# A transformer kernel on one core: the passage from its first block to its second, with norm factors applied behind the products, six weight slots from an earlier place, and the memory's operands made beside the gates

## The reference

```python
        x = x + y @ w_out[i]
        gate = jax.nn.sigmoid(rms_norm(x, ple_norm_g[i]) @ ple_w_gate[i])
        x = x + gate * (p[i] @ ple_w_proj[i])
    return rms_norm(x, final_norm_g)                 # end of the first block
...
        h = rms_norm_2(x, attn_norm[l])              # second block, layer 0: NSA attention
        proj = h @ w_in
...
    kv = (rms_norm_2(mem, g_mem) @ w_mem_kv).reshape(B, M, 2, N_MEM_HEADS, HEAD_DIM)   # for both layers
```

## Time and profile before

| | us |
|---|---|
| three runs | 1324.72, 1329.7, 1330.0; median 1329.7 |
| the profiled execution, its own time | 1329.96 |
| its span on the core | 1328.2 |
| TensorE busy in the span | 1142.6 |
| VectorE, ScalarE, GpSimd busy | 964.5, 692.3, 151.7 |
| mean granted TensorE clock | 0.924 of full speed |

### The profile page before, as it was taken

The page is one execution under the profiler, slowest core; times in us unless marked ns, Lnnn a source line. Parts: engine busy times, 40 slices in busy tenths (PEclk is TensorE's granted clock), DMA queues, the critical chain, the costliest instruction groups (busy, mean ns, idle before and its releaser), DMA issues.

```text
span 1328.2 us, 24918 instructions
## 1 busy us (share of the span) xinstructions
PE 1142.6 (86%) x10403; PEld 1062.7 (80%) x10403; DVE 964.5 (73%) x1722; ACT 692.3 (52%) x1261; POOL 151.7 (11%) x113
## 2 busy tenths in 40 slices
PE   6799876979799758948976699999999959999997
PEld 6688765969678748848965599999999848999997
DVE  5787954666778855577768867888867576788873
ACT  5642256555532366555345845565655274565562
POOL 2000000110000001142000001223110000123210
PEclk9999986989899967978986989999999879999999
DMA  8332110344231103415530034554556403455461
GB/s 340 127 100 93 65 64 1 135 151 157 90 128 66 65 1 142 139 69 186 179 128 25 1 129 157 173 177 159 199 203 211 150 1 101 156 173 175 159 207 63
DMA packets 24736, 167.54 MB, mean 126 GB/s; under 512 B 2737, under 2 KB 2865, under 8 KB 8497
## 3 DMA queue, kind: packets, MB, share of 16 engines
q1 hardware_dynamic: 24624, 165.96, 35.8%
HBM read 164.90 MB, written 1.05 MB: 125 GB/s over the span
## 4 chain that ended last, share of the span: by engine, by line
PE 48%; DVE 29%; ACT 17%; issue 4%; DMA 2%; POOL 0%; DVEq 0%; SPq 0%; ACTq 0%; POOLq 0%
PE ps L427 9%; PE ps L422 9%; PE ps L424 9%; DVE WL L381 8%; ACT WH L368 3%; DVE FR L381 3%; PE ps L445 3%; PE ps L453 3%; PE ps L447 3%; ACT ARENA L745 2%; PE ps L643 2%; DMA raw<-wst_in 2%; ACT FR L368 1%; ACT ARENA L2136 1%; ACT L484 1%
## 5 line engine op out<-in xcount | busy, mean ns | idle before, releaser
L381 DVE TENSOR_TENSOR WL<-raw,WH 128x1024 fp32r<-128x1024 f32 (+4 forms) x225 | 274.0, 1240 | 104.6 <-ACT WH L368 104.0
L422 PE MATMUL ps<-FR,WH 128*128 128x256 f32 x1248 | 305.3, 285 | 21.8 <-ACT WH L368 16.5
L424 PE MATMUL ps<-FR,WH 128*128 128x256 f32 x1248 | 301.2, 282 | 1.3 <-DVE FR L493 0.8
L368 ACT ACTIVATE WH<-raw 128x1024 fp32r<-128x1024 f32 (+4 forms) x225 | 218.3, 988 | 101.8 <-PE ps L427 55.4
L422 PEld LDWEIGHTS ps<-FR,WH 128*128 128x128 f32 x1248 | 240.4, 193 | 26.9 <-ACT WH L368 13.6
L424 PEld LDWEIGHTS ps<-FR,WH 128*128 128x128 f32 x1248 | 240.0, 192 | 3.2 <-DVE FR L493 1.9
L422 PE MATMUL ps<-FR,FR 128*128 128x256 f32 x680 | 169.1, 286 | 2.9 <-ACT FR L368 2.2
L427 PE MATMUL ps<-FR,WL 128*128 128x256 f32 x1248 | 170.1, 279 | 0.5 <-DVE WL L381 0.5
L424 PE MATMUL ps<-FR,FR 128*128 128x256 f32 x680 | 167.9, 284 | 0.2 <-DVE FR L493 0.2
L427 PEld LDWEIGHTS ps<-FR,WL 128*128 128x128 f32 x1248 | 155.7, 189 | 0.7 <-DVE WL L381 0.7
L381 DVE TENSOR_TENSOR FR<-raw,FR 128x1024 fp32r<-128x1024 f32 (+2 forms) x100 | 127.3, 1297 | 34.5 <-ACT FR L368 34.5
(11 more groups left out here) (320 smaller groups left out, 1825.9 us busy)
## 6 DMA issues: line engine op xcount, KB each, us to landing
raw<-wst_in SPq DMA_DIRECT2D x124, 1024.0 KB, 5.0
raw<-wst_in SPq DMA_DIRECT2D x14, 768.0 KB, 4.2
raw<-wst_in SPq DMA_DIRECT2D x11, 896.0 KB, 4.7
raw<-wst_in SPq DMA_DIRECT2D x4, 968.0 KB, 4.7
raw<-wst_in SPq DMA_DIRECT2D x2, 912.0 KB, 4.6
cst<-cst_in SPq DMA_DIRECT2D x1, 1681.0 KB, 15.3
X<-xT_in SPq DMA_DIRECT2D x2, 512.0 KB, 6.3
ARENA<-memT_in SPq DMA_DIRECT2D x1, 1024.0 KB, 4.8
```

The costliest lines, as they stand in the source:

```text
L368: a.activation(hi[:, 0:cols], src, ACT.Copy).then_inc(*put("split_hi", ("hi", i)))
L381: v.tensor_tensor(lo[:, 0:cols], src, hi[:, 0:cols].bitcast(F32), SUB).then_inc(*put("split_lo", ("lo", i)))
L422: pe.matmul(out, hv[:, k, :], src.hi[:, c, :], start=k0 == 0 and k == ks[0], stop=False)
L424: pe.matmul(out, hv[:, k, :], src.lo[:, c, :], start=False, stop=False)
```

## The change

1. **Factors behind the products.** The operand of the NSA projections is X times `g12`, the product of the two gains (final norm and attention norm), without row factors. It is split in the gate pairs of layer 1 (`HN`). The row factor of both norms, `rs12`, is multiplied in where the projections leave PSUM (as a column `rT12`, or as a row for `zc`). The memory's operands are M times its gain, its factor `mem_rs` is multiplied into the keys, and as a column into the values. Two small steps (`columns_pe`, `columns_v`) turn a row factor into a column. `scaled` is no longer used here, and GpSimd makes no parts.
2. **The memory's operands** for both layers are made in gate pairs 0 and 2 of layer 1: 16 `hi` on ScalarE, 16 `lo` on VectorE.
3. **Memory products first.** Keys of layer 0, mean of X, values of layer 0, keys of layer 1, second mean, values of layer 1, then the projections.
4. **Six slots** begin with the first `w_out` item of layer 1, before with the first item of the projections; so splits run 5 items ahead through `w_out` and the gates of layer 1.
5. **One `w_proj` item** of 1024 columns holds the weights of four outputs, in both layers; before, each output had its own of 256. The list of items has 314 entries in 157 tiles, before 326 in 159.
6. Buffers move in the arena: `M` lies at 2048, the operands at the end of `OutMap`.

```diff
-MORE_AT = ("mem v", 1)
+MORE_AT = ("gate", 1, 4)
...
+        if j < NW:
+            return w_slots[j], max(x for x in range(m - NW, m) if x % NW == j)
...
-        ahead = ahead or (2 if n < first_more() else 4 if event[0] == "cmp1" else NW + NMORE - 1)
+        ahead = ahead or (2 if n <= first_more() else 4 if event[0] == "cmp1" else NW + NMORE - 1)
...
-            if i == first_more():
+            if i == first_more() + NW:
                 for e in ("PE", "V", "G"):
-                    q.wait_ge(*got("end", "T", e))
+                    q.wait_ge(*got("end", ("L", 1), e))
...
+    def proj_pe(l, c0, ps):
+
+        if c0 % 4 == 0:
+            proj_item[0] = take(("ple_w_proj", l, tuple(r(128 * c0, 128 * c0 + 512)), 0, 2), 1024)
+        i, hi, lo = proj_item[0]
+        hv, lv = (x.rearrange("p (k m) -> p k m", k=2) for x in (hi, lo))
+        src, tag = p_parts[l], ("p", l)
+        qpe.wait_ge(*got("hi", i))
+        qpe.wait_ge(*got("lo", i))
+        for x in range(2):
+            o, m = ps[:, 256 * x:256 * x + 256], slice(128 * (c0 % 4 + x), 128 * (c0 % 4 + x) + 128)
+            for k in range(2):
+                qpe.wait_ge(*got("hi", tag, k))
+                pe.matmul(o, hv[:, k, m], src.hi[:, k, :], start=k == 0, stop=False)
+                qpe.wait_ge(*got("lo", tag, k))
+                pe.matmul(o, hv[:, k, m], src.lo[:, k, :], start=False, stop=False)
+                ins = pe.matmul(o, lv[:, k, m], src.hi[:, k, :], start=False, stop=k == 1)
+        ins.then_inc(*put("item_used", ("w_proj", l, c0), *([("used", i)] if c0 % 4 else [])))
+        B.at_items["w_proj", l, c0] = len(B.plan)
...
+        if l == 1 and c0 < 4:
+            for i in range(2):
+                for c in r(2 * c0, 2 * c0 + 4):
+                    part_x_lo(v, q, mem_parts[i], ("mem", i), c, vcol("mem_norm_2", i, 0, 8), M)
...
-            elif c0 == 4:
-                ps, free = psum("mem mean")
-                q.wait_ge(*got("mem y"))
-                newton(v, q, "mem_v", mem_rs, ps[:, 0:S], 1e-6, mem_hs[0], ("mem rs",), free)
-                q.wait_ge(*own("mem_v"))
-            elif c0 == 6:
-                for i in range(2):
-                    if i:
-                        q.wait_ge(*got("lo", ("mem", 0), 6))
-                        q.wait_ge(*got("lo", ("mem", 0), 7))
-                    scaled_v(v, q, M, vcol("mem_norm_2", i, 0, 8), mem_parts[i], ("mem", i), mem_hs, bank=mem_rs)
+            else:
+                if c0 == 0:
+                    v.tensor_tensor(g12, vcol("final_norm_g", None, 0, 8), vcol("attn_norm_2", 0, 0, 8), MUL).then_inc(*put("ple_v", ("g12",)))
+                q.wait_ge(*own("ple_v"))
+                for c in (c0, c0 + 1):
+                    part_x_lo(v, q, HN, "HN", c, g12)
...
-            if l == 1 and c0 == 4:
-                q.wait_ge(*got("mem mean"))
-                table(a, LNEXP)
-                ps, _ = psum("mem mean")
-                a.activation(mem_hs[0], ps[:, 0:S], ACT.Ln, bias=C("eps6")).then_inc(*put("mem_a"))
-                q.wait_ge(*own("mem_a"))
-                a.activation(mem_hs[0], mem_hs[0], ACT.Exp, scale=-0.5).then_inc(*put("mem_a", ("mem y",)))
+            if l == 1 and c0 < 4:
+                for i in range(2):
+                    for c in r(2 * c0, 2 * c0 + 4):
+                        part_x_hi(a, mem_parts[i], ("mem", i), c, vcol("mem_norm_2", i, 0, 8), M)
...
-            elif c0 < 4:
-                pass
-        if l == 1:
-            q.wait_ge(*got("mem mean"))
-            for c0 in range(0, 8, 2):
+            else:
+                q.wait_ge(*got("g12"))
+                for c in (c0, c0 + 1):
+                    part_x_hi(a, HN, "HN", c, g12)
+                if c0 == 4:
+                    q.wait_ge(*got("mem mean"))
                 a.activation(m.sq3[c0 // 2], X[:, c0:c0 + 2, :], ACT.Square).then_inc(*put("square", ("square", ("in", 2), c0)))
...
     def between_pe():
+        memory_k_pe(0)
         mean_mm(("in", 2), lo_[1].sq3[0])
-        memory_kv_pe(0)
+        memory_v_pe(0)
+        memory_k_pe(1)
+        columns_pe(mem_rs, "mem rT", "mem rs")
         mean_mm(("fin", 1), t_sq[0])
+        memory_v_pe(1)
+        columns_pe(rs12, "rT12", "rs12")
         B.mark("PE", "end", "T", "PE")
...
     def between_v(v, q):
         barrier(q, "V", ("O", 1))
-        rstd_v(v, q, ("in", 2), None, t_y0)
+        split_lo(v, q, "mem k", 0)
+        ps, free = psum("mem mean")
+        q.wait_ge(*got("mem y"))
+        newton(v, q, "mem_v", mem_rs, ps[:, 0:S], 1e-6, mem_y, ("mem rs",), free)
+        split_lo(v, q, "mem v", 0)
+        rstd_v(v, q, ("in", 2), rs1, t_y0)
         for c in range(KC):
-            v.scalar_tensor_tensor(X[:, c, :], X[:, c, :], vcol("final_norm_g", None, c), mean_bank[:, 0:S], MUL, MUL) \
-                .then_inc(*put("scaled", ("x fin", c), *([("mean free", ("in", 2))] if c == 7 else [])))
-        split_lo(v, q, "mem k", 0)
-        split_lo(v, q, "mem v", 0)
+            v.scalar_tensor_tensor(X[:, c, :], X[:, c, :], vcol("final_norm_g", None, c), rs1, MUL, MUL) \
+                .then_inc(*put("scaled", ("x fin", c)))
+        q.wait_ge(*got("mem rs"))
+        memory_k_v(v, q, 0)
+        split_lo(v, q, "mem k", 1)
+        columns_v(v, q, mem_rT, "mem rT")
+        split_lo(v, q, "mem v", 1)
+        rstd_v(v, q, ("fin", 1), rs12, t_y0)
+        v.tensor_tensor(rs12, rs12, rs1, MUL).then_inc(*put("rstd_v", ("rs12",)))
+        memory_k_v(v, q, 1)
+        columns_v(v, q, rT12, "rT12")
         B.mark("V", "end", "T", "V")
...
     def between_a(a, q):
         barrier(q, "A", ("O", 1))
+        ps, _ = psum("mem mean")
+        q.wait_ge(*got("mem mean"))
+        table(a, LNEXP)
+        a.activation(mem_y, ps[:, 0:S], ACT.Ln, bias=C("eps6")).then_inc(*put("mem_a"))
+        q.wait_ge(*own("mem_a"))
+        a.activation(mem_y, mem_y, ACT.Exp, scale=-0.5).then_inc(*put("mem_a", ("mem y",)))
+        split_hi(a, q, "mem k", 0)
         rstd_a(a, q, ("in", 2), t_y0)
-        split_hi(a, q, "mem k", 0)
+        split_hi(a, q, "mem v", 0)
         for c in range(0, KC, 2):
             q.wait_ge(*got("x fin", c + 1))
             a.activation(t_sq[c // 2], X[:, c:c + 2, :], ACT.Square).then_inc(*put("square", ("square", ("fin", 1), c)))
-        memory_kv_a(a, q, 0)
+        split_hi(a, q, "mem k", 1)
+        memory_v_a(a, q, 0)
+        split_hi(a, q, "mem v", 1)
+        rstd_a(a, q, ("fin", 1), t_y0)
+        memory_v_a(a, q, 1)
         B.mark("A", "end", "T", "A")
...
-        barrier(q, "V", "T")
-        split_lo(v, q, "mem k", 1)
-        rstd_v(v, q, ("fin", 1), None, m.zt[:, 0, 0:256])
-        scaled_v(v, q, X, vcol("attn_norm_2", 0, 0, 8), m.H, "HN", m.hs, ("fin", 1), mean_bank[:, 0:S])
-        split_lo(v, q, "mem v", 1)
...
+            v.tensor_scalar(dst, ps[:, 0:NSA_N[g]], rT12[:, 1:2], None, MUL).then_inc(*put("proj_v", ("zt n", g) if g < 2 else ("zv n", 1), free))
...
+            v.tensor_tensor(m.zc[:, c0:c0 + 2, :] if c0 < 4 else m.qm, two(ps), bc(rs12, 1, 2), MUL) \
+                .then_inc(*put("proj_v", ("zc a", c0) if c0 < 4 else ("qm",), free))
...
-        barrier(q, "A", "T")
-        split_hi(a, q, "mem k", 1)
-        rstd_a(a, q, ("fin", 1), m.zt[:, 0, 0:256])
-        scaled_a(a, q, m.H, "HN", m.hs)
-        memory_kv_a(a, q, 1)
+        q.wait_ge(*got("rT12", "v"))
```

108 lines of the change are left out of this document (57 added, 51 removed).

## The result

The changed kernel takes 1332.7 us (median of 18 runs, 1330.3 to 1335.2), the kernel before 1329.7 in the same runs (18, 1324.7 to 1333.4): ratio 1.0023, 95% interval 1.0013 to 1.0032. It is 3.0 us slower (1.7 to 4.3), a small loss, outside the -0.4 us that was forecast. The profiled execution took 1331.15 us, of which 1329.1 are span.

A forecast was written before the change was run, and what follows sets the result against it. TensorE was taken as the bound, waiting on VectorE and ScalarE's chain before the projections. Passage -1.6, U +1.2 and layer 0 at 0 gave -0.4 us: 1329.3 as median, range 1324 to 1335 (whole 1319 to 1339).

The forecast's parts named there:

- The paragraph on w_out of layer 1: Layer 1's w_out: five splits ahead, one behind a late tile; first and fourth sums 5.7 us late, bounds nothing and 8.
- Late tile, first sum at 521.3: Layer 1's w_out: tile behind the memory load lands at 519.0, hi and lo follow, first sum 5.7 us late.
- the rival that a harmless tile would give 5.7 back: Layer 1's w_out: no hold, gates 5.7 earlier, no slow restart (1.5); 1322 us; chance 0.28 together with high clock.
- First gate pair 557.0, last add 583.9: Layer 1's gates: x of pair 0 8.7 us late, other three pairs 26.9 together; the gates lose 10.5.
- lo and sums meet in pair 0: Layer 1's first gate pair: memory's lo and GpSimd's sums collide, up to 4.3 us, 1333.6; no chance of its own.
- First projection 618.3: Passage: chain of memory factors, values, scaling and sums lets projections start at 618.3 instead of 619.89, 1.6 us earlier.
- The rival by the same rule: Passage: scaling X from SBUF excludes GpSimd, one sum (1.4 us) on top, 1330.7; no chance of its own.
- U +1.2: Behind the projections: VectorE's zc copy stands before U, so U and compression are 1.2 us later (0 to 3).
- Layer 0 at 0: Layer 0's gates: the 3.54 us w_proj wait goes, a shorter one comes behind; 0, bounds -1 and +2.3.
- The rival "the clock": Values and projections: pauses of about 5, 10 and 5 us keep TensorE's clock low; 1339 us; chance 0.18.

The follow-up runs named there:

- e2_mem_later: The changed kernel with only the memory load issued two tiles later in SyncE's queue: 1328.2 us, ratio 0.9986.
- e11_oldmap: The best kernel (all edits, 1312.8 us) with only the changed kernel's map of slots put back: 1320.3 us, ratio 0.9915.
- e6_pairs24: The changed kernel with slots in old turn and memory load two tiles later, plus memory's parts moved to gate pairs 2 and 4: 1317.7 us, ratio 0.9911.
- e12_l0_items: The best kernel (all edits, 1312.8 us) with layer 0's w_proj items put back to one per output: 1314.6 us, ratio 0.9885.

## Why the prediction was wrong

*The step that failed* is one that the sum doesn't have. The paragraph on w_out of layer 1 starts from the mixer's end of before, and takes that end as given. The new rule for the first slots was costed for what comes behind it, five splits ahead, and not for the two items in front of which it puts a new wait. The numbers were at hand: 86 mod 3 is 2, so the splits of items 86 and 87 wait one item longer, 2.8 us each, 5.6 together. The runs show 5.6 to 5.9 at the place (from the split of item 85 to that of item 87, changed kernel and `e2_mem_later` against the old turn) and 4.0 to 4.2 in `e11_oldmap`, and 5.7 to 7.5 up to the split of item 88. With 5.6 the sum would have been +5.2 instead of -0.4; 3.0 was measured. That the time fell inside the range given is no merit of the mechanism: a loss that the sum did not have was made smaller by gains that it did not have either (below).

The other steps, on the changed kernel's own base (3.1 us later from 511.5 on):

- *Late tile, first sum at 521.3*: 524.38 - 3.08 = 521.3. The wait for the load is there (4.77 us), and against the two splits of before the 5.7 are right (10.91 less 5.24 from the split of item 88). But not all of it was the tile's: without the wait for it only 4.1 of it goes, for five splits in a row then hold the sum for the other 1.6, and that the sum left out. So the rival that a harmless tile would give 5.7 back was too generous. The Trainium skill ("DMA: Bandwidth & Descriptors", Queues, rings and completion order) has each engine take descriptors in ring order, but lets a later one finish its write before an earlier one, so that the tile "can't pass" the memory's load is more than it says; the runs show that with the load behind it the tile is not waited for.
- *First gate pair 557.0, last add 583.9*: 559.86 - 3.08 = 556.8, and 586.5 - 3.1 = 583.4. Right, though the eight lo took 5.43 us and not 3.3: ScalarE's squares, hi and table load, as forecast, end with the sigmoid at 557.8, and the lo at 558.5, so all but 0.7 of it is hidden. That lo and sums meet in pair 0 had been a rival; `e6_pairs24` shows that they do. With the rule of the Trainium skill ("SBUF — State Buffer", Who interferes with whom) the trace agrees in kind: here VectorE was the one that paid (3.24 to 5.43), and the sums took 4.17 beside the lo and 4.16 without.
- *First projection 618.3*: 619.70 - 3.08 = 616.6. Values 592.1 for 592.6; X is scaled at 601.2 for 601.1, squares and sums took 6.8 and not 8.1, near the lower bound given. The rival by the same rule (one sum, 1.4 us, on top) did not come in this execution: the scaling took 4.29 us, but the sums only 4.43. In three later runs, one of them the same kernel as a run with 4.46, the sums took 5.66 us and squares and sums together 8.1, as forecast (last section). So 6.8 instead of 8.1 is one of two outcomes, which the prediction gave as its lower bound and could not tell from the other.
- *U +1.2*: the last copy could only start with its product, at 658.85, and U began 0.61 behind that, where it began 0.48 ahead of it before: 1.1 later against the products. But the projections took 1.7 us less than before to this product (39.15 instead of 40.82), which I had at nothing. A second missing term: TensorE comes out of the values of layer 1 with a pause of 1.5 us only, and its granted clock is 1.00 from 615 to 660, where the projections had 0.96.
- *Layer 0 at 0*: -1.3 in the profile (w_out and gates) and 0 in the medians of `e12_l0_items`. The wait came behind, as said: 3.3 us before the third w_proj pair instead of 3.54 before the second.

The sum of the two traces is then: -2.7 up to the new slots in layer 1's mixer (1.7 by the end of layer 0, 1.0 in the mixer's first part, which has no edit), +5.8 in the slots and behind them, -3.3 to the first projection, -1.7 in the projections, +1.1 for U, +1.7 behind 1066 us (last section): +0.9, the difference of the two spans (1329.1 and 1328.2). The rival "the clock" had its pauses right and not its price.

## What to carry to other kernels

Where a ring of buffers changes its size in mid-program, write out for the first items on either side which use each of them waits for: one position off is one item's time, in a stretch that the change doesn't touch otherwise. When you cost a wait, ask what the waiting engine would be late for without it; here five splits stood behind a tile, and of the 5.7 us that held the first sum only 4.1 came off with the tile. And in a passage where TensorE waits for two engines in turn, put first what frees a bank or starts the next chain, and last what waits for TensorE: a few lines moved gave 6.3 us at the place and 5.5 in the medians (0.9931 to 0.9890). With all the edits the kernel takes 1312.8 and 1314.3 us in two measurements, 0.9885 of the kernel before.
